# A causal attention stage whose longest row tile is turned by DMA instead of by TensorE

## The chip, the cores and the metric

The kernel runs on one core of a Trainium2 chip. The metric is the device time of one execution in microseconds (us), lower is better. The core has five engines that work through their own instruction lists in order and wait for each other only through semaphores: TensorE (PE: matmuls, and PEld: its weight loads), VectorE (DVE), ScalarE (ACT), GpSimd (POOL) and SyncE (SP), whose queue issues nearly all DMAs here.

## The reference

Two layers over 1024 tokens of width 1024, batch 1. Layer 0 mixes a pooling branch and a short convolution. Layer 1 is attention with 16 heads, and it is the part that matters here:

```python
def causal_attention(q, k, v):          # q, k: 16 heads of 96; v: 16 heads of 64
    def block(i):                       # 8 blocks of 128 query rows
        s = jnp.einsum('bqhd,bkhd->bhqk', qb, k) * scale
        s = jnp.where(k_idx[None, :] <= q_idx[:, None], s, -jnp.inf)
        p = jax.nn.softmax(s, axis=-1)
        return jnp.einsum('bhqk,bkhd->bqhd', p, v)
...
    o = causal_attention(q, k, v)
    return x + (o * jax.nn.silu(z)) @ w_out
```

Values are float32. The kernel reaches that precision with pairs of 16-bit numbers: a value is split into a high half (the value rounded to float16) and a low half (what the rounding lost), and a product takes two or three passes.

## The kernel before, in words

The program has a front part (layer 0 and the input projections), then the projections of queries, keys and values, then attention, then the output projection. Attention works on 16 heads one after the other; a head has 8 query tiles of 128 rows. By the causal mask tile i needs only the first i+1 blocks of 128 keys, so tile 7 is 1024 columns wide and tile 0 is 128. Within a head the tiles come in the order `ORDER = (7, 3, 6, 2, 5, 1, 4, 0)`; n counts tiles over all heads (n = 8h is tile 7 of head h), so big tiles (i of 4 and more, `heads_probs_big`) and small ones (`heads_probs_small`) alternate. A big tile's row is cut into two pieces of up to 512 columns, a small tile has one.

One tile passes through these stages, each written on its engine's list:

- PE, `score_tile(n)` (L111 to L113): scores into PSUM, three passes.
- DVE, `maxima(n)` (L2487): scales, adds the mask, writes the row to SBUF (`heads_probs_big` or `_small`) and takes the row's maximum.
- ACT, `exponentials(n)` (L2357): the exponential in place, with the row's sum.
- PE, `transposes(n, k)` (L2729): piece k in blocks of 128x128 float32, against the identity, into one of three PSUM banks.
- ACT, `high(n, k)` (L2366): the piece from PSUM to `heads_pt_hi`, float16.
- DVE, `low(n, k)` (L2495): PSUM minus that, to `heads_pt_lo`, float16.
- PE, `product(n, k)` (L2747, L2748): both halves against V, two matmuls for each block of 128.

The order is written out by hand, and no scheduler changes it. In step n PE does the scores of tile n+2, the transposes of tile n and the product of tile n-2, ACT does `high` of tile n and then `exponentials` of tile n+2, and DVE does `maxima` of tile n+2 and then `low` of tile n:

```python
for n in range(N + BEHIND):                     # ACT
    for k in range(len(pieces(tile_of(n)[1]))):
        high(n, k)
    exponentials(n + AHEAD)                     # AHEAD = 2
...
for n in range(N + BEHIND + TURN_LAG + 1):      # DVE
    maxima(n + AHEAD)
    for k in range(len(pieces(tile_of(n)[1]))):
        low(n, k)
```

After each two heads PE also turns their outputs (`turn`, L2756, eight transposes of `heads_o_pair`) and DVE multiplies them into the gate (L2508). ACT copies each group of four tiles' outputs out of PSUM (`copy_out`, L2373), and POOL sums and scales them (L2642, L2647), splits V (L2633, L2635) and, from the middle of attention on, prepares operands of the output projection. SP issues for head h, once the scores of head h-2 are done, two DMA transposes that bring the keys and the queries of the head from DRAM (`load_k`, L2275, `load_q`, L2278), then weights, V and stores.

## Time and profile before

| | |
|---|---|
| median of 3 runs | 964.08 us (963.87 to 965.23) |
| the profiled execution | 965.27 us, its span 963.4 us |
| granted TensorE clock over the span | 0.998 |
| attention, about 656 to 881 us of the span | 226 us |
| PE, DVE, ACT busy over the whole span | 98%, 84%, 60% |
| DMA | 103.67 MB |

The span runs from the first to the last instruction; 1.9 us of the profiled execution's time lie around it. Busy time is the time in which at least one instruction of an engine is under way. Durations of matmuls overlap their neighbours (their ends are modelled), and the last 0.1 us of a DVE or ACT instruction overlaps the next one; what an instruction costs its queue is therefore read from the start of one instruction to the start of the next, called its slot below. In a row of the timeline "x2" merges two neighbours.

### The profile page before, as it was taken

The page shows a single profiled execution, that of the slowest core. Times are in us where ns is not written, and L with a number is a line of the kernel's source. Part 1 is how long each engine was busy: PE and PEld are TensorE (multiplying, and loading weights), DVE is VectorE, ACT ScalarE, POOL GpSimd, SP SyncE. Part 2 cuts the span into 40 slices and gives each one's busy share as a digit, 9 for nine tenths or more (in the row PEclk, how much of TensorE's full clock was granted, in tenths as well). Part 3 has the DMA queues.
Part 4 walks back from the last instruction along what each step waited for, and adds up shares of the span by engine and source line. Part 5 has one row for each costly group of instructions (what it writes and reads, how often), then busy time and mean ns, then how long its engine had stood idle before and what let it go on. Part 6 is the DMA issues. An engine that isn't in the chain of part 4 may idle for free.

```text
span 963.4 us, 16135 instructions
## 1 busy us (share of the span) xinstructions
PE 947.1 (98%) x5830; PEld 668.9 (69%) x5830; DVE 813.5 (84%) x1410; ACT 579.5 (60%) x1076; POOL 376.3 (39%) x425
## 2 busy tenths in 40 slices
PE   9999999999999999999998999999999999999998
PEld 7788544444688888544456999997778888887443
DVE  5798899899865579989786799998999999998763
ACT  7434544434444354555646788866999999998230
POOL 0002243222000002235402567867673589897220
PEclk9999999999999999999999999999999999999999
DMA  9320431111055422423024164557665766460231
GB/s 305 46 58 23 110 86 46 44 45 45 1 183 163 134 66 66 132 88 79 9 72 132 44 208 146 203 176 203 116 161 146 172 153 111 92 175 2 88 110 66
DMA packets 165343, 103.67 MB, mean 108 GB/s; under 512 B 75272, under 2 KB 149520, under 8 KB 165008
## 3 DMA queue, kind: packets, MB, share of 16 engines
q1 hardware_dynamic: 159216, 102.25, 37.8%
q10 hardware_dynamic: 6048, 0.39, 0.5%
q8 instruction: 47, 0.77, 0.3%
q14 instruction: 32, 0.26, 0.1%
HBM read 56.48 MB, written 29.36 MB: 89 GB/s over the span
## 4 chain that ended last, share of the span: by engine, by line
PE 64%; DVE 24%; POOL 5%; issue 4%; ACT 3%; DVEq 0%; POOLq 0%; ACTq 0%
PE banks L111 18%; PE banks L113 18%; PE banks L112 17%; PE banks L2729 5%; PE banks L2747 2%; DVE heads_y L2478 2%; PE banks L2748 1%; DVE heads_x L2473 1%; DVE heads_x L2474 1%; DVE heads_ss L2520 1%; DVE front_lt L1231 1%; ACT front_set_b L722 1%; DVE heads_probs_big L2487 1%; DVE front_l L1231 1%; DVE heads_last_y L2478 1%
## 5 line engine op out<-in xcount | busy, mean ns | idle before, releaser
L2495 DVE TENSOR_TENSOR heads_pt_lo<-banks,heads_pt_hi 128x512 f16<-128x512 f32 (+2 forms) x192 | 102.1, 554 | 11.3 <-ACT heads_pt_hi L2366 7.0
L2366 ACT ACTIVATE heads_pt_hi<-banks 128x512 f16<-128x512 f32 (+2 forms) x192 | 88.3, 484 | 4.9 <-PE banks L2729 4.6
L2747 PE MATMUL banks<-heads_v,heads_pt_hi 128*128 128x128 f16 x576 | 74.5, 220 | 0.0
L2729 PE MATMUL banks<-ident,heads_probs_big 128*128 128x128 f32 x416 | 69.1, 279 | 1.4 <-ACT heads_probs_big L2357 1.3
L2748 PE MATMUL banks<-heads_v,heads_pt_lo 128*128 128x64 f16 x576 | 69.5, 193 | 0.0
L2487 DVE CUSTOM_DVE_ANT_0 heads_probs_big<-banks,heads_mask,score_scale 128x1024 f32<-128x1024 f32 (+1 forms) x64 | 68.5, 1071 | 0.9
L2357 ACT ACTIVATE heads_probs_big<-heads_probs_big,heads_neg_max 128x1024 f32<-128x1024 f32 (+1 forms) x64 | 63.4, 991 | 5.5 <-DVE heads_neg_max L2487 3.6
L111 PE MATMUL banks<-front_act_hi,front_w_hi 128*128 128x512 f32 x160 | 63.9, 399 | 0.3 <-DVE front_w_lo L951 0.3
L111 PE MATMUL banks<-heads_k_t,heads_q_t 96*128 96x512 f16 (+2 forms) x192 | 62.9, 327 | 0.9 <-DVE heads_neg_max L2487 0.9
L113 PE MATMUL banks<-front_act_hi,front_w_lo 128*128 128x512 f32 x160 | 62.4, 390 | 0.0
L112 PE MATMUL banks<-front_act_lo,front_w_hi 128*128 128x512 f32 x160 | 62.3, 389 | 0.0
L112 PE MATMUL banks<-heads_k_t,heads_q_t 96*128 96x512 f16 (+2 forms) x192 | 62.3, 324 | 0.0
L113 PE MATMUL banks<-heads_k_t,heads_q_t 96*128 96x512 f16 (+2 forms) x192 | 61.5, 325 | 0.0
L626 POOL TENSOR_TENSOR front_left_first<-front_raw_first 128x512 f32<-128x512 f32 x1 | 1.3, 1297 | 147.8 <-DVE front_lt L1231 147.8
L2747 PEld LDWEIGHTS banks<-heads_v,heads_pt_hi 128*128 128x128 f16 x576 | 54.2, 99 | 0.7
L2748 PEld LDWEIGHTS banks<-heads_v,heads_pt_lo 128*128 128x128 f16 x576 | 51.3, 98 | 2.3
L2729 PEld LDWEIGHTS banks<-ident,heads_probs_big 128*128 128x128 f32 x416 | 46.7, 141 | 7.7 <-DVE heads_pt_lo L2495 3.3
L111 PE MATMUL banks<-front_y_hi,front_w_hi 128*128 128x512 f32 x128 | 50.0, 391 | 0.0
L113 PE MATMUL banks<-front_y_hi,front_w_lo 128*128 128x512 f32 x128 | 49.8, 389 | 0.0
L112 PE MATMUL banks<-front_y_lo,front_w_hi 128*128 128x512 f32 x128 | 49.8, 389 | 0.0
L626 POOL TENSOR_TENSOR front_x<-front_raw 128x512 f32<-128x512 f32 x7 | 9.7, 1380 | 85.6 <-DVE front_set_b L1090 36.5
L2357 ACT ACTIVATE heads_probs_small<-heads_probs_small,heads_neg_max 128x512 f32<-128x512 f32 (+1 forms) x64 | 35.9, 561 | 7.4 <-DVE heads_neg_max L2487 6.6
(488 smaller groups left out, 3099.7 us busy)
## 6 DMA issues: line engine op xcount, KB each, us to landing
qk_scratch<-heads_y SPq DMA_DIRECT2D x22, 512.0 KB, 3.6
front_x<-in_x_t SPq DMA_DIRECT2D x16, 512.0 KB, 5.2
front_raw<-in_w_in_ab SPq DMA_DIRECT2D x14, 512.0 KB, 5.1
qk_scratch<-heads_last_y SPq DMA_DIRECT2D x10, 512.0 KB, 3.6
front_w<-in_w_out_ab SPq DMA_DIRECT2D x8, 512.0 KB, 3.7
x_scratch<-front_x SPq DMA_DIRECT2D x8, 512.0 KB, 4.0
v_scratch<-heads_v SPq DMA_DIRECT2D x32, 128.0 KB, 3.0
heads_v_st<-v_scratch SPq DMA_DIRECT2D x8, 512.0 KB, 5.2
```

The lines of the kernel that those rows point to most:

```text
L111: nc.tensor.matmul(out, w_hi, a_hi, start=first, stop=False, skip_group_check=resumed)
L112: nc.tensor.matmul(out, w_hi, a_lo, start=False, stop=False, skip_group_check=resumed)
L113: return nc.tensor.matmul(out, w_lo, a_hi, start=False, stop=last, skip_group_check=resumed)
L1231: nc.vector.scalar_tensor_tensor(right_split(c, part, 1), right_source(c, part), later_scale[:, 0:1], right_split(c, part, 0), ALU.mult, A ...
L2357: nc.scalar.activation(row, row, ACT.Exp, bias=neg_max[:, h % 2, i:i + 1], scale=-1.0, accum_out=total[:, h % 2, i:i + 1]).then_inc(exp_do ...
L2366: nc.scalar.activation(pt_hi[:, q % PIECES, :width], t_ps[:, banks[("piece", n, k)] % 3, :width], ACT.Copy).then_inc(pt_high, 1)
L2478: nc.vector.tensor_tensor(y_slot(w)[:, :, :, P:P + QKH], x_slot(w), y_slot(w)[:, :, :, :QKH], ALU.subtract).then_inc(y_low, 1)
L2487: nc.vector.tensor_tensor_reduce(probs(n, 0, width), scores(i, 0, width), mask[:, S - width:], score_scale[:], 3e38, ALU.add, ALU.min, neg ...
L2495: nc.vector.tensor_tensor(pt_lo[:, q % PIECES, :width], t_ps[:, banks[("piece", n, k)] % 3, :width], pt_hi[:, q % PIECES, :width], ALU.sub ...
L2729: last = nc.tensor.transpose(t_ps[:, b, r * P:(r + 1) * P], probs(n, j * P, (j + 1) * P), ident[:])
L2747: nc.tensor.matmul(out, pt_hi[:, q % PIECES, blk], v2[e][:, j, :], start=(j == 0), stop=False)
L2748: last = nc.tensor.matmul(out[:, :VH], pt_lo[:, q % PIECES, blk], v2[e][:, j, :VH], start=False, stop=(j == i))
```

## The change

For tile 7 of each head but the first (n = 8, 16, ..., 120, fifteen tiles) the four stages after the exponential are replaced. ACT casts the whole row, 1024 columns, from SBUF to SBUF (`big_high`, to `out.big[0]`), right after the row's exponential. DVE subtracts it from the row, SBUF to SBUF (`big_low`, to `out.big[1]`), one step later. SP issues a DMA transpose for each half (`turn_big`), from SBUF to SBUF, behind the loads of the keys and queries of the next head. PE multiplies the result with V in one go (`big_product`) five steps after the tile's own step, where it was two and in two pieces. The ring of transposed pieces has 5 places where it had 6, the buffers of the output projection are placed elsewhere, the four residual rows load only after the last scores, and POOL's waits within its own operations use one shared semaphore.

```diff
+        def turn_big(h):
+            for part, made in enumerate((out.big_high, out.big_low)):
+                sp.wait_ge(made, h)
+                if h > 1:
+                    sp.wait_ge(out.big_done, h - 1)
+                sp.dma_start_transpose(out.big_t[part][:], out.big[part][:].rearrange("p b k -> p (b k)")
+                                       ).then_inc(out.big_in, 16)
...
             sp.wait_ge(s_ready, NT * (h - 1))
             load_k(h)
             load_q(h)
+            turn_big(h - 1)
...
+        turn_big(HEADS - 1)
+        sp.wait_ge(s_ready, N)
         for m in range(out.PLACES_OF_ROWS):
             out.load_residual(sp, m)
...
+        def big_high(n):
+            h = n // NT
...
+            act.wait_ge(exp_done, n + 1)
+            act.wait_ge(out.big_in, 32 * (h - 1))
+            nc.scalar.activation(out.big[0][:].rearrange("p b k -> p (b k)"), probs(n, 0, S), ACT.Copy).then_inc(out.big_high, 1)
...
             if n + AHEAD < N:
                 exponentials(n + AHEAD)
+                if by_queue(n + AHEAD):
+                    big_high(n + AHEAD)
...
-            if n >= 4:
-                dve.wait_ge(pt_ready, piece_no(n - 4, len(pieces(tile_of(n - 4)[1])) - 1) + 1)
+            if n >= 4 and by_queue(n - 4):
+                dve.wait_ge(out.big_low, (n - 4) // NT)
+            elif n >= 4:
+                dve.wait_ge(pt_ready, piece_base[n - 3])
...
+        def big_low(n):
+            h = n // NT
+            dve.wait_ge(out.big_high, h)
+            dve.wait_ge(out.big_in, 32 * (h - 1))
+            nc.vector.tensor_tensor(out.big[1][:].rearrange("p b k -> p (b k)"), probs(n, 0, S),
+                                    out.big[0][:].rearrange("p b k -> p (b k)"), ALU.subtract).then_inc(out.big_low, 1)
...
             if n < N:
-                for k in range(len(pieces(tile_of(n)[1]))):
+                for k in range(len(parts(n))):
                     low(n, k)
+                if by_queue(n + 1) and n + 1 < N:
+                    big_low(n + 1)
                 if n % 4 == 3:
                     inverse(n // 4)
...
+        def big_product(n):
+            h = n // NT
+            e, o_part = h % 2, o_ps[:, n // 4 % 2, o_slot(NT - 1), :]
+            pe.wait_ge(out.big_in, 32 * h)
+            for j in range(NT):
+                nc.tensor.matmul(o_part, out.big_t[0][:, j], v2[e][:, j, :], start=(j == 0), stop=False)
+                last = nc.tensor.matmul(o_part[:, :VH], out.big_t[1][:, j], v2[e][:, j, :VH], start=False, stop=(j == NT - 1))
+            last.then_inc(out.big_done, 1)
...
+                if k == 0 and by_queue(big) and big < N:
+                    big_product(big)
```

`by_queue(n)` is true for n = 8, 16, ..., 120, and `parts(n)` is then empty. Two places of the lists show what moves.

DVE, at the border of two heads, the change (`heads_probs_big` of 128x1024 is tile 7, of 128x896 tile 6, `heads_probs_small` of 128x512 tile 3, of 128x384 tile 2; the rows called ISA are `maxima` and the reading of its maximum). The list starts after `maxima` of tile 7, with `low` of tile 4 of the head before:

```order
L2528 TENSOR_TENSOR heads_pt_lo<-banks,heads_pt_hi 128x512
L2528 TENSOR_TENSOR heads_pt_lo<-banks,heads_pt_hi 128x128
L2520 ISA heads_probs_small,heads_neg_max<-banks,heads_mask,score_scale 128x512
L2520 ISA heads_neg_max 128x1
L2528 TENSOR_TENSOR heads_pt_lo<-banks,heads_pt_hi 128x128
L2535 TENSOR_TENSOR out_big_lo<-heads_probs_big_260,out_big 128x1024
L2543 RECIPROCAL heads_inv<-heads_total 128x2x2
L2520 ISA heads_probs_big_270,heads_neg_max<-banks,heads_mask,score_scale 128x896
L2520 ISA heads_neg_max 128x1
L2520 ISA heads_probs_small,heads_neg_max<-banks,heads_mask,score_scale 128x384
L2520 ISA heads_neg_max 128x1
L2528 TENSOR_TENSOR heads_pt_lo<-banks,heads_pt_hi 128x512
```

The same place before:

```order
L2495 TENSOR_TENSOR heads_pt_lo<-banks,heads_pt_hi 128x512
L2495 TENSOR_TENSOR heads_pt_lo<-banks,heads_pt_hi 128x128
L2487 ISA heads_probs_small,heads_neg_max<-banks,heads_mask,score_scale 128x512
L2487 ISA heads_neg_max 128x1
L2495 TENSOR_TENSOR heads_pt_lo<-banks,heads_pt_hi 128x128
L2503 RECIPROCAL heads_inv<-heads_total 128x2x2
L2487 ISA heads_probs_big_267,heads_neg_max<-banks,heads_mask,score_scale 128x896
L2487 ISA heads_neg_max 128x1
L2495 TENSOR_TENSOR heads_pt_lo<-banks,heads_pt_hi 128x512 x2
L2487 ISA heads_probs_small,heads_neg_max<-banks,heads_mask,score_scale 128x384
L2487 ISA heads_neg_max 128x1
L2495 TENSOR_TENSOR heads_pt_lo<-banks,heads_pt_hi 128x512
```

The two `low` of tile 7 are gone from between the maxima of tiles 6 and 2, and the new subtraction stands ahead of the maxima of tile 6.

ACT, the same border, the change: exponential of tile 7, the cast, `high` of tile 0 of the head before, the exponentials of tiles 3 and 6, `high` of tile 3, the exponential of tile 2:

```order
L2375 ACTIVATE heads_probs_big_260,heads_total<-heads_probs_big_260,heads_neg_max 128x1024
L2394 ACTIVATE out_big<-heads_probs_big_260 128x1024
L2384 ACTIVATE heads_pt_hi<-banks 128x128
L2375 ACTIVATE heads_probs_small,heads_total<-heads_probs_small,heads_neg_max 128x512
L2375 ACTIVATE heads_probs_big_270,heads_total<-heads_probs_big_270,heads_neg_max 128x896
L2384 ACTIVATE heads_pt_hi<-banks 128x512
L2375 ACTIVATE heads_probs_small,heads_total<-heads_probs_small,heads_neg_max 128x384
```

The same place before:

```order
L2357 ACTIVATE heads_probs_big_257,heads_total<-heads_probs_big_257,heads_neg_max 128x1024
L2366 ACTIVATE heads_pt_hi<-banks 128x128
L2357 ACTIVATE heads_probs_small,heads_total<-heads_probs_small,heads_neg_max 128x512
L2366 ACTIVATE heads_pt_hi<-banks 128x512 x2
L2357 ACTIVATE heads_probs_big_267,heads_total<-heads_probs_big_267,heads_neg_max 128x896
L2366 ACTIVATE heads_pt_hi<-banks 128x512
L2357 ACTIVATE heads_probs_small,heads_total<-heads_probs_small,heads_neg_max 128x384
```

The cast has come in front of `high` of tile 0, and the two casts of tile 7's pieces have gone.

## Rows read from the trace of the kernel before

**Rows 1.** The page: the span, and busy time of PE and DVE.

```profile
span 963.4 us, 16135 instructions
PE 947.1 (98%) x5830; PEld 668.9 (69%) x5830; DVE 813.5 (84%) x1410; ACT 579.5 (60%) x1076; POOL 376.3 (39%) x425
```

**Rows 2.** Windows: attention, then two neighbouring heads of it.

```profile
655.90:881.50 225.60, 221.62 (x2360) 176.22 (x2359) 211.78 (x515) 207.04 (x493) 172.62 (x199) 1.00 0.59 137
773.40:786.50 13.10, 13.10 (x147) 10.52 (x145) 12.35 (x30) 12.60 (x32) 12.63 (x12) 1.00 0.56 122
786.50:800.40 13.90, 13.90 (x153) 11.23 (x152) 13.32 (x32) 12.48 (x31) 10.94 (x11) 1.00 0.64 150
```

**Rows 3.** Timeline of DVE: start us, us, instruction [idle before <-releaser].

```profile
773.44 1.28 DVE L2487 CUSTOM_DVE_ANT_0 heads_probs_big<-banks,heads_mask,score_scale 128x1024 f32<-128x1024 f32 x1
...
774.65 0.88 DVE L2495 TENSOR_TENSOR heads_pt_lo<-banks,heads_pt_hi 128x512 f16<-128x512 f32 x2
...
775.45 0.74 DVE L2487 CUSTOM_DVE_ANT_0 heads_probs_small<-banks,heads_mask,score_scale 128x512 f32<-128x512 f32 x1
...
776.21 0.29 DVE L2495 TENSOR_TENSOR heads_pt_lo<-banks,heads_pt_hi 128x128 f16<-128x128 f32 x1
...
776.60 1.15 DVE L2487 CUSTOM_DVE_ANT_0 heads_probs_big<-banks,heads_mask,score_scale 128x896 f32<-128x896 f32 x1
...
777.68 1.49 DVE L2495 TENSOR_TENSOR heads_pt_lo<-banks,heads_pt_hi 128x512 f16<-128x512 f32 x2
...
779.09 0.61 DVE L2487 CUSTOM_DVE_ANT_0 heads_probs_small<-banks,heads_mask,score_scale 128x384 f32<-128x384 f32 x1
...
779.99 0.69 DVE L2495 TENSOR_TENSOR heads_pt_lo<-banks,heads_pt_hi 128x512 f16<-128x512 f32 x1 [0.28 <-ACT heads_pt_hi L2366]
...
786.51 1.28 DVE L2487 CUSTOM_DVE_ANT_0 heads_probs_big<-banks,heads_mask,score_scale 128x1024 f32<-128x1024 f32 x1
...
789.78 0.29 DVE L2495 TENSOR_TENSOR heads_pt_lo<-banks,heads_pt_hi 128x128 f16<-128x128 f32 x1
```

**Rows 4.** Timeline of ACT, the same columns and heads.

```profile
774.77 1.15 ACT L2357 ACTIVATE heads_probs_big<-heads_probs_big,heads_neg_max 128x1024 f32<-128x1024 f32 x1
...
775.92 0.25 ACT L2366 ACTIVATE heads_pt_hi<-banks 128x128 f16<-128x128 f32 x1
...
778.34 1.03 ACT L2357 ACTIVATE heads_probs_big<-heads_probs_big,heads_neg_max 128x896 f32<-128x896 f32 x1
...
779.37 0.58 ACT L2366 ACTIVATE heads_pt_hi<-banks 128x512 f16<-128x512 f32 x1
...
787.84 1.15 ACT L2357 ACTIVATE heads_probs_big<-heads_probs_big,heads_neg_max 128x1024 f32<-128x1024 f32 x1
```

**Rows 5.** Timeline of PE, the same columns, an earlier and the same head.

```profile
764.11 0.63 PE L2729 MATMUL banks<-ident,heads_probs_big 128*128 128x128 f32 x4
...
764.58 0.22 PE L2747 MATMUL banks<-heads_v,heads_pt_hi 128*128 128x128 f16 x1
...
771.47 0.39 PE L2729 MATMUL banks<-ident,heads_probs_small 128*128 128x128 f32 x2
...
771.94 0.38 PE L111 MATMUL banks<-heads_k_t,heads_q_t 96*128 96x512 f16 x1
```

**Rows 6.** Sources and tiles: durations ns min/median/max of SBUF operations on DVE and ACT.

```profile
L960 DVE TENSOR_TENSOR front_w_lo<-front_w,front_w_hi x15: 1211/1218/1471, 58.0 to 372.2; 128x1024 fp32r<-128x1024 f32 x15
L1816 ACT ACTIVATE heads_dump<-gate x8: 1055/1056/1122, 526.6 to 594.4; 128x1024 bf16<-128x1024 f32 x8
```

**Rows 7.** Groups by form, 520 to 680 us, POOL busy too: busy us, mean ns.

```profile
L2478 DVE TENSOR_TENSOR heads_y<-heads_x,heads_y 128x768 f16<-128x768 f32 x16 | 19.2, 1203 | 2.1 <-ACT heads_y L2351 2.1
```

**Rows 8.** Timeline of SP's queue in the next head, and landing times of the keys.

```profile
784.72 1.91 SPq L2275 DMA_TRANSPOSE heads_k_t<-qk_scratch  x1
786.68 2.20 SPq L2278 DMA_TRANSPOSE heads_q_t<-qk_scratch  x1
DMA to landing us min/median/max: 4.3/5.1/6.4
```

More of the change, by code:

```diff
@@ L1716, in __init__ @@
         self.w_row, self.w_size, self.w_scale, self.unscale = [field(self.OUT_PAIRS) for _ in range(4)]
-        sum_places = (joint.rstd_at, ring_at + tile, ring_at + 4 * tile)
-        self.sums = [[at(f"sums{q}_{n}", block, F32, place + (n if q or n < 3 else 2) * half)[:]
-                      for n in range(4) if q or n != 2]
+        sum_places = (spare + 6 * 1024, joint.rstd_at, ring_at + 4 * tile)
+        self.sums = [[at(f"sums{q}_{n}", block, F32, place + (n if q == 2 or n < 3 else 2) * half)[:]
+                      for n in range(4) if q == 2 or n != 2]
                      for q, place in enumerate(sum_places)]
-        self.sums[0].insert(2, self.quarter_of(0, 1, 0))
+        for q in range(2):
+            self.sums[q].insert(2, self.quarter_of(q, 1, 0))
         self.left = [at(f"left{q}", [P, FORMS, 2] + block[1:], F16, w_place + q * FORMS * half) for q in range(self.OUT_PAIRS)]
@@ L1877, in pool_t @@
         one, other = self.t_terms(c, f, raw, raw)
-        self.nc.gpsimd.tensor_tensor(raw, one, other, ALU.subtract).then_inc(self.t_staged, 1)
-        pool.wait_ge(self.t_staged, done + 1)
-        self.nc.gpsimd.tensor_copy(hi, raw).then_inc(self.t_cast, 1)
-        pool.wait_ge(self.t_cast, done + 1)
+        link(self.nc.gpsimd.tensor_tensor(raw, one, other, ALU.subtract))
+        link(self.nc.gpsimd.tensor_copy(hi, raw))
         self.nc.gpsimd.tensor_tensor(lo, raw, hi, ALU.subtract).then_inc(self.t_split, 1)
@@ L2188, in pieces, with by_queue, parts @@
         return [range(b, min(b + 4, i + 1)) for b in range(0, i + 1, 4)]
-    PER_HEAD = sum(len(pieces(i)) for i in range(NT))
+    def by_queue(n):
+        return n > 0 and n % NT == 0
+    def parts(n):
+        return [] if by_queue(n) else pieces(tile_of(n)[1])
+    piece_base = [0]
+    for n in range(N):
+        piece_base.append(piece_base[-1] + len(parts(n)))
     def piece_no(n, k):
-        h, p = divmod(n, NT)
-        return PER_HEAD * h + sum(len(pieces(ORDER[x])) for x in range(p)) + k
+        return piece_base[n] + k
     def turn_step(pair, c):
@@ L2367, in high @@
                                  ACT.Copy).then_inc(pt_high, 1)
+        def big_high(n):
+            h = n // NT
+            if h == 1:
+                for e in range(VSLOTS):
+                    act.wait_ge(v_stored[e], 16 * len(range(e, UNITS, VSLOTS)))
+            act.wait_ge(exp_done, n + 1)
+            act.wait_ge(out.big_in, 32 * (h - 1))
+            nc.scalar.activation(out.big[0][:].rearrange("p b k -> p (b k)"), probs(n, 0, S), ACT.Copy).then_inc(out.big_high, 1)
         def copy_out(g):
+            if g % 2 == 0 and g:
+                act.wait_ge(out.big_done, g // 2)
             act.wait_ge(pv_done, piece_no(4 * g + 3, len(pieces(ORDER[(4 * g + 3) % NT])) - 1) + 1)
@@ L2412, in scalar @@
             if n < N:
-                for k in range(len(pieces(tile_of(n)[1]))):
+                for k in range(len(parts(n))):
                     high(n, k)
@@ L2541, in vector @@
             if n < N:
-                for k in range(len(pieces(tile_of(n)[1]))):
+                for k in range(len(parts(n))):
                     low(n, k)
+                if by_queue(n + 1) and n + 1 < N:
+                    big_low(n + 1)
                 if n % 4 == 3:
@@ L2691, in gpsimd @@
                 for n in range(2):
-                    out.pool_t(pool, c, 2 * late + n)
+                    out.pool_t(pool, link, c, 2 * late + n)
                 if not late:
-                    out.pool_gate(pool, c + 2)
+                    out.pool_gate(pool, link, c + 2)
             if h == 11:
@@ L2735, in product @@
             q = piece_no(n, k)
-            if n % NT == 0 and k == 0:
+            first = 1 if by_queue(n - 1) else 0
+            if n % NT == first and k == 0:
                 pe.wait_ge(v_low, h + 1)
-            if n % 4 == 0 and k == 0:
+            if n % 4 == (first if n % NT < 2 else 0) and k == 0:
                 if g >= 2:
@@ L2801, in tensor @@
             old = n - BEHIND
-            new_pieces = len(pieces(tile_of(n)[1])) if n < N else 0
-            old_pieces = len(pieces(tile_of(old)[1])) if 0 <= old < N else 0
+            new_pieces = len(parts(n)) if n < N else 0
+            old_pieces = len(parts(old)) if 0 <= old < N else 0
+            big = n - BIG_BEHIND
             if n == N:
```

54 lines of the change are left out of this document (27 added, 27 removed).

## The prediction

> **What bounds the kernel now.** I read the page first: the span is 963.4 us and PE is busy in 98% of it [rows 1]. Then the windows of attention, because the change touches nothing else: 225.6 us, of which PE is busy 221.6, DVE 211.8 and ACT 207.0 [rows 2]. The two windows of one head each are what to look at. A head in which no outputs are turned lasts 13.1 us, one in which they are 13.9, and in both PE is busy all of it. But DVE is busy 12.35 and 13.32 of them, and ACT 12.60 and 12.48 [rows 2]. So PE sets the pace, with DVE only 0.6 to 0.75 us of a head behind it. A change that takes time from PE can give at most those 0.6 to 0.75 us a head before DVE is the bound, and it gives less if it makes DVE wait.
>
> So the third view is the timeline of DVE through one head border [rows 3]. The reader is to see how dense it is: maxima of tile 7 at 773.44, `low` of tile 4 at 774.65, maxima of tile 3 at 775.45, `low` of tile 0 at 776.21, maxima of tile 6 at 776.60, the two `low` of tile 7 at 777.68, maxima of tile 2 at 779.09, and only then a wait of 0.28, for ACT. Each `low` needs a cast of ACT, and that cast stands behind an exponential that needs a maximum of DVE. The two engines hand work to and fro, and it goes without waits only because each has other work while the other has the tile. For tile 7 that other work is what the change removes or lengthens.
>
> **PE.** Removed: eight transposes in each of 15 tiles. Four take a slot of 0.47 us (764.11 to 764.58) [rows 5], so 0.94 a head and 14.1 in all. The products are the same sixteen matmuls, moved: nothing. This is a gain only where PE is the bound.
>
> **ACT.** Removed: two casts of 512 columns out of PSUM, with slots of 0.48 (779.37 to the next instruction) to 0.62 [rows 3, 4]. Added: one cast of 1024 columns in SBUF. The nearest row is a one-input operation over the same shape, 1.056 us [rows 6], and with 0.1 of overlap a slot of 0.96. Its sum stays; its place doesn't: it now stands between the exponential of tile 7 and `high` of tile 0.
>
> **DVE.** Removed: the two `low` of tile 7, a slot of 1.41 (777.68 to 779.09), and the wait of 0.28 behind them [rows 3]. Added: a subtraction of 1024 columns in SBUF. The nearest row is 1.218 us for 1024 columns of float32 and a rounded copy [rows 6], a slot of 1.14. Upper bound: while POOL works, 768 columns took 1.203 on average [rows 7] where that rate gives 0.91, a factor of 1.32, so up to 0.38 more. I take 1.14, since the maker of that row is the same operation.
>
> **Wait X, in front of `low` of tile 0.** Before, ACT begins the exponential of tile 7 at 774.77 and `high` of tile 0 at 775.92 [rows 4], and DVE finds it done at 776.21 [rows 3]. With the cast between, ACT is done at 774.77 + 1.15 + 0.96 + 0.25 and some 0.05 for the semaphore, 777.18. DVE waits 0.97 us. In a head with turned outputs DVE has a gate product more and comes to that `low` at 789.78 [rows 3], while ACT began at 787.84 [rows 4] and is done at 790.25: 0.47. Queued behind it are the new subtraction and the maxima of tile 6.
>
> **Wait Y, in front of `low` of tile 3.** Before, between the maxima of tile 6 and of tile 2 DVE had the 1.41 us of tile 7's pieces, and ACT had time for the exponential of tile 6 (1.03, 778.34 to 779.37) and `high` of tile 3 (0.62 until DVE takes it at 779.99) [rows 3, 4]. Now DVE goes from the maxima of tile 6 straight to those of tile 2 (0.62) and then needs `high` of tile 3, which is behind that exponential. From the end of the maxima: 0.12 until ACT starts (774.65 to 774.77 for tile 7) + 1.03 + 0.62 = 1.77, less 0.62, is 1.15 us of waiting.
>
> **Wait Z, in front of the next tile 7.** PE's product of tile 7 (eight blocks; three take 0.25 of the 0.47 us between 771.47 and 771.94, so 0.66) now stands right before the 1024 columns of scores, in step n+5 [rows 5]. DVE wants these scores. Between 0, if PE is ahead, and 0.66; I take 0.3, since PE has to catch up after each wait of DVE.
>
> **The sum.** No outputs turned: -1.41 - 0.28 + 1.14 + 0.97 + 1.15 + 0.3 = +1.87 a head. Outputs turned: the same with 0.47 for X, +1.37. The turned outputs of a pair fall into heads 3, 5, ..., 15, seven of the fifteen: 8 x 1.87 + 7 x 1.37 = 24.6 us. Made against the profiled execution (965.27, its span 963.4) that is 989.9, and against the median of 964.08, which lies 1.2 below it, 988.7. I predict 989.
>
> **The transposes in the DMA queue.** The sum needs them in time. Counted from the start of the maxima of tile 7: the cast ends at 3.4 (774.77 + 1.15 + 0.96 - 773.44) and the subtraction at 5.1 (777.18 + 0.20 + 1.14 - 773.44). SP is free by then: the two loads of the next head are issued from 784.72 to 788.88 [rows 8], 2.4 after maxima that start at 786.51 [rows 3], one period of 13.07 on. A load of 1024x256 takes 4.3 to 6.4 us from issue to landing, 5.1 in the middle [rows 8], and each new transfer has half its bytes: the low half has landed 10.2 to 11.5 after the maxima. PE wants it where it ends the transposes of tile 1, 1.75 us before the next such maxima (771.69 against 773.44) [rows 3, 5]: with the stretched period at 13.07 + 1.57 - 1.75 = 12.9. Hidden, by 1.4 to 2.7 us; in a head with turned outputs the product comes 0.4 later still. No row shows a transpose whose source is SBUF, so how long it takes is the open point, and its bounds are in the rivals.
>
> The Trainium skill speaks against the change here: "VectorE: DVE Perf Modes", section "The three transpose paths", gives a block of 128x128 1309 ns by the DMA crossbar and 390 ns on TensorE. By it the sixteen blocks of a tile would take 20.9 us one after the other, land 11.4 us late in each head, and make about 1160 us, an estimate from that page. The trace doesn't agree for the same instruction from DRAM: a load holds sixteen such blocks and has landed after 5.1 us [rows 8]. No row shows an SBUF source. I give it 1 in 100.
>
> **What costs nothing.** The loads of weights and V now stand behind both transposes in SP's queue, some 3 us later than their 788.88; V is for a head that starts one period later, and without that cover each us late would be a us of PE. The ring of 5 pieces holds the four of two tiles and one more. POOL's semaphores change their names, not their number of waits. The residual rows are wanted only by the additions after attention, under the first output products.
>
> **Rivals.**
> - *PE stays the bound* (faster, 950): the waits X and Y are filled. It decides at X + Y + Z = 0.55 a head (1.41 + 0.28 - 1.14); below that DVE gains. For it: PE's 100% [rows 2]. Against it: DVE's list is in order, and X alone is 0.97. 964 - 14.1 = 950. 7 in 100.
> - *Nothing is left of it* (962 to 966): X and Y are half as long, because ACT gets ahead in the rest of the head. Against it: both start at a maximum of DVE, so ACT can't be ahead. 5 in 100.
> - *The transposes come late as well* (997 to 1040): if the two don't overlap, the low half lands at 3.4 + 2 x 5.1 = 13.6, which is 0.7 late in a head without turned outputs and 0.3 in the other, about 8 us in all, 997; with 6.4 each, 3.2 late and 48 more, 1037. The skill's figure would be beyond. 10 in 100, with 1010 in the middle.
> - *The forecast*: 78 in 100. Its own range: X and Y each 0.2 shorter and Z 0 takes 10.5 off, 978; Z 0.66 and POOL's 0.38 add 11.1, 1000.
>
> **Range and chances.** 975 to 1008 holds the forecast's range with a little on both sides and the nearer half of the late transposes; left out are the faster and the equal case and the later half, with some of the forecast's tails. About 2 us (0.2%) is what a measurement of this kernel can tell from no change. Faster 0.07, same 0.05, slower 0.88.
>
> **What the profile after would show.** PE no longer busy all of a head window, a head of about 14.9 us without and 15.3 with turned outputs; on DVE a wait of about 1 us for ACT before `low` of tile 0 and another before `low` of tile 3; the new subtraction near 1.2 us; PE waiting for DVE's maxima and ACT's exponentials, not for the transfers. I am wrong if DVE's waits for ACT stay as short as now and heads fall under 13.1 us, or if PE sits in front of the product of tile 7.

## The result, and the profile after

The changed kernel takes 1003.04 us (median of 4, 1001.92 to 1003.54), the kernel before beside it on the same chip 964.62 (963.87 to 965.23): a ratio of 1.0396, 95% interval 1.0384 to 1.0408. It is 38.4 us slower. Forecast were 24.6 us more, 989, and a range of 975 to 1008, which holds it. The profiled execution has a span of 1000.1 us, against 963.4 [rows 1]: 36.7 more. It is less than 38.4 because the profiled execution of the changed kernel was its fastest, 1001.92, and that of the kernel before was slower than its median, 965.27.

The page of the changed kernel, the span, the busy time, and four of the five groups of PE, DVE and ACT in attention in front of which most idle time stands (last two numbers: idle us before the group, and the releaser of most of it; the fifth is ACT's `high`, 11.4 us, nearly all for PE's transposes):

```profile
span 1000.1 us, 15913 instructions
PE 952.4 (95%) x5710; PEld 663.4 (66%) x5710; DVE 815.0 (81%) x1395; ACT 579.9 (58%) x1061; POOL 386.3 (39%) x425
...
L2528 DVE TENSOR_TENSOR heads_pt_lo<-banks,heads_pt_hi 128x512 f16<-128x512 f32 (+3 forms) x162 | 81.6, 529 | 36.2 <-ACT heads_pt_hi L2384 33.2
L111 PE MATMUL banks<-heads_k_t,heads_q_t 96*128 96x512 f16 (+2 forms) x192 | 64.8, 338 | 24.1 <-DVE heads_neg_max L2520 23.7
L2375 ACT ACTIVATE heads_probs_big<-heads_probs_big,heads_neg_max 128x1024 f32<-128x1024 f32 (+1 forms) x64 | 63.4, 990 | 41.4 <-DVE heads_neg_max L2520 39.2
L2520 DVE CUSTOM_DVE_ANT_0 heads_probs_big<-banks,heads_mask,score_scale 128x1024 f32<-128x1024 f32 (+1 forms) x64 | 68.6, 1072 | 11.1 <-PE banks L113 10.7
```

PE is no longer busy all the time, and the three engines wait for one another: DVE's `low` for ACT, ACT and PE for DVE's `maxima`, and the `maxima` for PE's scores. Nobody in this list waits for a transfer.

The windows of one head each, from one start of the maxima of tile 7 to the next (they answer to [rows 2]):

```profile
758.32:773.62 15.30, 13.03 (x138) 9.42 (x137) 12.08 (x29) 12.83 (x30) 8.70 (x9) 1.00 0.84 170
773.62:789.52 15.90, 13.79 (x146) 10.37 (x145) 13.28 (x32) 12.55 (x29) 5.94 (x8) 1.00 0.76 167
789.52:806.18 16.66, 14.10 (x138) 10.72 (x137) 13.01 (x30) 12.45 (x29) 16.15 (x12) 0.90 0.69 126
806.18:822.86 16.68, 15.01 (x146) 11.76 (x145) 13.48 (x32) 12.46 (x29) 10.71 (x11) 0.90 0.74 162
```

The first number behind the window is its length, the next four busy times are those of PE, weight loads, DVE and ACT, the fifth is POOL's, and then stands the granted clock. A head takes 15.30 us without and 15.90 with turned outputs, where it took 13.07 and 14.00. But half of the heads are longer still, 16.2 to 16.8, and in them TensorE was granted only 0.89 to 0.90 of its clock.

The timeline of DVE in the second of these heads, with turned outputs (it answers to [rows 3]):

```profile
773.62 1.28 DVE L2520 CUSTOM_DVE_ANT_0 heads_probs_big<-banks,heads_mask,score_scale 128x1024 f32<-128x1024 f32 x1 [0.76 <-PE banks L113]
...
777.48 0.29 DVE L2528 TENSOR_TENSOR heads_pt_lo<-banks,heads_pt_hi 128x128 f16<-128x128 f32 x1 [0.50 <-ACT heads_pt_hi L2384]
777.68 1.22 DVE L2535 TENSOR_TENSOR out_big_lo<-heads_probs_big,out_big 128x1024 f16<-128x1024 f32 x1
...
780.55 0.61 DVE L2520 CUSTOM_DVE_ANT_0 heads_probs_small<-banks,heads_mask,score_scale 128x384 f32<-128x384 f32 x1
781.09 0.08 DVE L2520 DVE_READ_ACCUMULATOR2_ANT heads_neg_max<- 128x1 f32 x1
782.31 0.69 DVE L2528 TENSOR_TENSOR heads_pt_lo<-banks,heads_pt_hi 128x512 f16<-128x512 f32 x1 [1.15 <-ACT heads_pt_hi L2384]
```

All three waits of the forecast are there: Z in front of the maxima of tile 7 (0.76), X in front of `low` of tile 0 (0.50; 1.10 in the head before it, without turned outputs), and Y in front of `low` of tile 3 (1.15). X in the head before it:

```profile
762.18 0.29 DVE L2528 TENSOR_TENSOR heads_pt_lo<-banks,heads_pt_hi 128x128 f16<-128x128 f32 x1 [1.10 <-ACT heads_pt_hi L2384]
```

ACT shows why, in the head of the timeline above:

```profile
774.95 1.15 ACT L2375 ACTIVATE heads_probs_big<-heads_probs_big,heads_neg_max 128x1024 f32<-128x1024 f32 x1
776.00 0.19 ACT L2375 ACTIVATION_READ_ACCUMULATOR heads_probs_big<-heads_probs_big,heads_neg_max 128x1 f32 x1
776.22 1.06 ACT L2394 ACTIVATE out_big<-heads_probs_big 128x1024 f16<-128x1024 f32 x1
777.19 0.26 ACT L2384 ACTIVATE heads_pt_hi<-banks 128x128 f16<-128x128 f32 x1
...
780.66 1.04 ACT L2375 ACTIVATE heads_probs_big<-heads_probs_big,heads_neg_max 128x896 f32<-128x896 f32 x1 [2.52 <-DVE heads_neg_max L2520]
```

The new cast (L2394) stands between the exponential of tile 7 and `high` of tile 0, for which DVE waits. Then, behind the exponential of tile 3, ACT itself sits idle for 2.52 us until the maxima of tile 6.

### The profile page after: what moved, and what is told of

Read it like the earlier page. It is cut to its first block, busy times and chain, and to the rows that moved or that the text cites. A ratio compares the mean times of both kernels' runs of the same rounds, so it can differ in the third digit from the quotient of the medians.

```text
span 1000.1 us, 15913 instructions
## 1 busy us (share of the span) xinstructions
PE 952.4 (95%) x5710; PEld 663.4 (66%) x5710; DVE 815.0 (81%) x1395; ACT 579.9 (58%) x1061; POOL 386.3 (39%) x425
## 4 chain that ended last, share of the span: by engine, by line
PE 53%; DVE 25%; POOL 9%; issue 8%; ACT 4%; DVEq 0%; POOLq 0%; ACTq 0%
PE banks L111 16%; PE banks L113 16%; PE banks L112 16%; PE banks L2772 3%; DVE heads_probs_big L2520 2%; DVE heads_y L2509 2%; DVE heads_x L2504 1%; DVE heads_x L2505 1%; PE banks L2791 1%; POOL out_t_hl L1880 1%; POOL out_pool_stage L1878 1%; DVE heads_ss L2560 1%; DVE front_lt L1231 1%; POOL heads_o_sum L2684 1%; POOL out_gate_hl L1862 1%
## 5 line engine op out<-in xcount | busy, mean ns | idle before, releaser
L2528 DVE TENSOR_TENSOR heads_pt_lo<-banks,heads_pt_hi 128x512 f16<-128x512 f32 (+3 forms) x162 | 81.6, 529 | 36.2 <-ACT heads_pt_hi L2384 33.2
L2384 ACT ACTIVATE heads_pt_hi<-banks 128x512 f16<-128x512 f32 (+3 forms) x162 | 71.0, 463 | 11.4 <-PE banks L2772 11.0
L2791 PE MATMUL banks<-heads_v,heads_pt_hi 128*128 128x128 f16 x456 | 59.7, 223 | 0.0
L2772 PE MATMUL banks<-ident,heads_probs_big 128*128 128x128 f32 x296 | 52.6, 302 | 4.9 <-ACT heads_probs_big L2375 3.5
L2792 PE MATMUL banks<-heads_v,heads_pt_lo 128*128 128x64 f16 x456 | 55.6, 195 | 0.0
L2684 POOL TENSOR_TENSOR heads_o_sum<-heads_o_raw 128x256 f32<-128x256 f32 x32 | 24.3, 759 | 59.7 <-ACT heads_o_raw L2402 58.9
L2772 PEld LDWEIGHTS banks<-ident,heads_probs_big 128*128 128x128 f32 x296 | 37.2, 153 | 12.9 <-DVE heads_pt_lo L2528 4.9
L2791 PEld LDWEIGHTS banks<-heads_v,heads_pt_hi 128*128 128x128 f16 x456 | 43.9, 101 | 1.7
L2792 PEld LDWEIGHTS banks<-heads_v,heads_pt_lo 128*128 128x128 f16 x456 | 41.5, 99 | 2.7
L111 PEld LDWEIGHTS banks<-heads_k_t,heads_q_t 96*128 96x128 f16 x192 | 19.2, 100 | 36.2 <-DVE heads_neg_max L2520 27.7
```

The costliest lines, as they stand in the source:

```text
L111: nc.tensor.matmul(out, w_hi, a_hi, start=first, stop=False, skip_group_check=resumed)
L2384: nc.scalar.activation(pt_hi[:, q % PIECES, :width], t_ps[:, banks[("piece", n, k)] % 3, :width], ACT.Copy).then_inc(pt_high, 1)
L2528: nc.vector.tensor_tensor(pt_lo[:, q % PIECES, :width], t_ps[:, banks[("piece", n, k)] % 3, :width], pt_hi[:, q % PIECES, :width], ALU.sub ...
L2684: nc.gpsimd.tensor_tensor(o_sum[:, g % 2], raw[:, :, :VH], raw[:, :, VH:], ALU.add).then_inc(o_summed, 1)
L2772: last = nc.tensor.transpose(t_ps[:, b, r * P:(r + 1) * P], probs(n, j * P, (j + 1) * P), ident[:])
L2791: nc.tensor.matmul(out, pt_hi[:, q % PIECES, blk], v2[e][:, j, :], start=(j == 0), stop=False)
```

## Experiments

All kernels were timed beside the kernel before, whose medians were 964.2 to 965.2 us there. "Heads" are the distances between the maxima of tile 7, first without and then with turned outputs. Of each kernel the shortest that recur are given, at a granted clock of 1.00; other heads of the same kernel are longer, and where that matters it is said.

### Both new instructions at the old places

```
 scalar:  for k in range(len(parts(n))): high(n, k)
+         if by_queue(n): big_high(n)
          exponentials(n + AHEAD)
-         if by_queue(n + AHEAD): big_high(n + AHEAD)
 vector:  for k in range(len(parts(n))): low(n, k)
-         if by_queue(n + 1) and n + 1 < N: big_low(n + 1)
+         if by_queue(n): big_low(n)
```

> The cast of the whole row goes to the place in ACT's list where the two casts of tile 7's pieces stood (before the exponential of tile 6), the subtraction to the place in DVE's list where the two low stood (after the maxima of tile 6). Transposes by the queue, their bytes and PE's savings stay. Theory A (DVE and ACT wait for each other because the cover is gone: X in front of low of tile 0, Y in front of low of tile 3): both waits fall under 0.4 us, a head comes down from 15.3/15.9 to 13.0 to 13.6 / 13.9 to 14.2, PE stays busy enough to keep its clock at 1.00, and the time is 960 to 974. Theory B (transposes from SBUF cost the time, by late landing or by loading the DMA engines): the halves are made 1.5 to 2 us later than in the changed kernel, so it gets no better, 1000 or more, and PE waits in front of the product of tile 7.

979.54 us (978.12 to 981.08), ratio 1.0151 (1.013 to 1.0172). Heads of 13.73 and 14.34, X and Y are gone, the clock is 1.00 in each head:

```profile
719.75:733.48 13.73, 12.66 (x138) 9.47 (x137) 12.29 (x30) 13.07 (x31) 5.99 (x7) 1.00 0.69 151
733.48:747.82 14.34, 13.67 (x146) 10.33 (x145) 13.28 (x31) 13.18 (x31) 4.29 (x5) 1.00 0.88 205
```

Most of the loss, 23.5 of 38.4 us, was in where the two instructions stand. But the expectation was too low by 6 at its upper end: without X and Y a head still isn't shorter than before. Nine of 14 heads are longer than these two, up to 15.11 us. Part of that is the subtraction: it takes 1.22 us in the undisturbed heads and up to 2.13 in others, 3.9 us more in all fifteen together than at 1.22.

### Only the subtraction at its old place

The second half of the diff above, alone.

> Only the subtraction goes back to its old place on DVE; the cast stays right behind the exponential. Theory A: Y (1.15 a head) is filled by the subtraction, X (0.5 to 1.0 a head) stays. 15 heads x 1.15 less, some 17 us, and more where PE's clock no longer falls: 975 to 988. Theory B: the low half is made 2 us later, nothing gained or slower: 1003 or more.

983.08 us (981.27 to 984.5), ratio 1.0184 (1.0165 to 1.0202), inside the 975 to 988 expected. Y is down to 0.20, X is still 1.10 and 0.50; heads of 14.33 and 14.93:

```profile
721.57:735.90 14.33, 13.03 (x138) 9.43 (x137) 12.17 (x29) 13.17 (x31) 6.39 (x8) 1.00 0.66 148
```

Y was worth 0.97 a head, 14.5 in all, where 1.15 was expected, and with it the drops of the clock went.

### Only the cast one step later

```
 scalar:  for k in range(len(parts(n))): high(n, k)
+         if by_queue(n + 1) and n + 1 < N: big_high(n + 1)
          exponentials(n + AHEAD)
-         if by_queue(n + AHEAD): big_high(n + AHEAD)
```

> Only the cast moves, by one place: behind high of tile 0 in ACT's list. The subtraction stays in front of the maxima of tile 6. Theory A: X moves from low of tile 0 to the subtraction and is 0.2 shorter at most, Y stays at 1.15: 998 to 1003, nearly no change. A rival within A, that X comes from the place of the cast alone: 15 x 0.5 to 1.0 less, 988 to 995.

998.71 us (995.85 to 1000.01), ratio 1.0343 (1.032 to 1.0365). X is gone, but without turned outputs DVE now waits 0.65 for the cast itself, in front of the subtraction. Heads of 14.95 and 15.55, 0.35 less. So this move alone gives a third of the 0.97 that X was put at, since the wait partly moves to the next hand-over, as theory A had it. With the subtraction out of the way the same move of the cast gives more, as the fifth experiment shows.

### PE filled where it was idle

```
 score_tile:
-    for kc in range(i // 4 + 1):
+    for kc in [0] * (3 if by_queue(n - 3) else 0) + list(range(i // 4 + 1)):
```

> The changed kernel with three more rounds of the scores of tile 2 (three passes of 384 columns each, 1.47 us in all, the same values written again) where PE sat idle for 1.57 us before the scores of tile 5. It is more work for PE. Theory C (the 12 us beyond the forecast are half the granted clock, which fell to 0.50 for some 3.5 us in seven heads, after PE had been idle in them): the clock stays at 1.00, the heads of 16.1 to 16.8 us come down to 15.3 and 15.9, and the time is 994 to 999, faster with more work. If the clock is only a symptom: 1003 or slower, by up to 0.2 us a head.

999.38 us (998.37 to 1000.5), ratio 1.0354 (1.0337 to 1.0371): 3.7 us less than the changed kernel, with more work on PE, and just above the 994 to 999 expected. No head has a lower clock any more. The head with the largest gain and the two that went the other way:

```profile
694.83:710.13 15.30, 14.30 (x147) 10.39 (x146) 12.17 (x29) 13.07 (x31) 14.33 (x20) 1.00 0.80 189
710.13:727.52 17.39, 15.25 (x155) 11.23 (x154) 14.86 (x31) 13.07 (x31) 8.39 (x12) 1.00 0.67 151
...
821.95:838.23 16.28, 14.30 (x147) 10.39 (x146) 13.06 (x30) 12.55 (x29) 15.44 (x16) 1.00 0.76 129
```

The first was 16.24 and is 15.30, the clean value. The other two were 16.82 and 15.40: in them DVE is busy 14.86 and 13.06, and the subtraction takes 2.71 and 2.19 us, where it takes 1.22 at 777.68 in the changed kernel, with POOL idle. In the head of 17.39 an operation of POOL on 768 columns begins at 714.18:

```profile
714.20 2.71 DVE L2535 TENSOR_TENSOR out_big_lo<-heads_probs_big,out_big 128x1024 f16<-128x1024 f32 x1
```

So two things, seen apart here, make a head longer than 15.30 or 15.90: a lower clock behind PE's idle time, and a subtraction that runs beside POOL.

### The cast ahead of the exponential, the subtraction at its old place

The cast as in the third experiment and the subtraction as in the second.

> The changed kernel with both new instructions at other places: the cast stands right behind `high` of the tile before (tile 0), ahead of the exponential of tile 3 and not behind that of tile 7's neighbour, and the subtraction stands where the two `low` of tile 7 stood. Theory A (the places of the two make the waits X and Y; the sum of ACT's and DVE's work alone does not): X and Y stay away as in the run with the old places (979.5), and `low` of tile 0 no longer waits at all while the exponentials behind it start 0.96 us later; the hand-over after tile 7 is the best of the three, so 974 to 980. Rival (the busy time of ACT, 13.04 of 13.70 us in a head of that run, is now what bounds): the order inside ACT changes nothing, 979 to 982.

980.73 us (977.96 to 981.92), ratio 1.0161 (1.0143 to 1.0179). Heads of 13.38 and 14.34:

```profile
722.68:736.06 13.38, 12.45 (x138) 9.47 (x137) 12.29 (x30) 13.05 (x31) 6.36 (x8) 1.00 0.70 163
```

Beside the second experiment only the cast has moved, and X is gone with no wait for the cast in its place: 0.95 a head without turned outputs (14.33 to 13.38) and 0.59 with them (14.93 to 14.34). That is the whole of X, 0.97 and 0.47 in the forecast. Beside the old places (the first experiment) the head without turned outputs gains 0.35, and others lose it again (one has 16.34), so theory A isn't borne out in the time: the medians, 980.7 and 979.5, don't differ clear of their spread.

### The high half turned twice

```
 turn_big:
+    for again in range(2 - part):
+        if again: sp.wait_ge(out.big_in, 48 * h - 32)
         sp.dma_start_transpose(...)
```

> The changed kernel, but the high half of each tile 7 is transposed twice by the queue, the second time when the first has landed; the low half goes behind both. Theory A (the transposes are hidden: the low half lands about 5 us before PE's product of it): both halves land some 3 us later, still about 2 us early, so no change, 1001 to 1005. Rival (part of the missing 13 us is the queue: PE or the later loads wait for it in heads that the chain of waits does not show): each head later by up to 3 us, 1008 to 1045.

1001.59 us (1000.3 to 1004.5), ratio 1.0385 (1.0365 to 1.0406), as the changed kernel. In the changed kernel the product starts 7.1 to 9.0 us after the low half is issued. Here it starts 3.2 to 7.0 us after it, on average 3 us less, and it waited for it 0.3 us in two heads together. So the transfers are hidden in the changed kernel: landing takes 3.0 to 3.4 of its 7.1 us or more.

### PE's product one step earlier

```
-    AHEAD, BEHIND, TURN_LAG, PIECES, BIG_BEHIND = 2, 2, 5, 5, 5
+    AHEAD, BEHIND, TURN_LAG, PIECES, BIG_BEHIND = 2, 2, 5, 5, 4
```

> The changed kernel with PE's product of tile 7 one step earlier, at n+4 and not n+5, so that it no longer stands right before the 1024 columns of scores of the next tile 7. Theory A (wait Z is the product, 0.33 to 0.96 us a head): DVE finds those scores ready and the product runs in PE's idle time, 15 heads x 0.35 to 0.7 = 5 to 10 us less, 992 to 998. Rival (PE comes to those scores late because it has caught up after DVE's waits, and everything in front of them counts, wherever the product stands): no change, 1001 to 1005.

1005.64 us (1004.1 to 1007.31), ratio 1.0424 (1.0408 to 1.0439). Theory A falls: heads of 15.31 and 15.90, nothing gained, and nine heads with a lower clock where seven had one. PE waits 0.40 for the exponential of tile 5 at the start of step n+4 and from there works without a gap to the scores of the next tile 7; the product counts at either place.

### The product in front of that wait

`BIG_BEHIND` is 3, and the waits for V and for the copied outputs stand in front of the product of tile 7.

> The changed kernel with PE's product of tile 7 in step n+3 and not n+5 (the waits for V and for the copied outputs move with it). With the product at n+4 nothing was gained, because PE works without a gap from its wait for the exponential of tile 5 (the transposes at 769.48, in front of the old place and the new) to the scores of the next tile 7, so that 0.66 us counts in either. Step n+3 lies in front of that wait. Theory A (Z is the product inside that stretch): the waits in front of the maxima of tile 7 fall by 0.3 to 0.6 and the heads by 0.3 to 0.5, 996 to 1000, if the low half, which lands 8.4 us after the maxima, is in time. Rival (what PE gains there it loses in front of the scores of tile 1, or at the transfer): 1001 to 1008.

1002.39 us (1001.06 to 1006.14), ratio 1.039 (1.0368 to 1.0412). Where the clock is 1.00 the heads are 0.68 shorter, as much as the product takes; the whole isn't:

```profile
742.00:758.68 16.68, 15.00 (x146) 11.75 (x145) 13.48 (x31) 13.17 (x31) 6.06 (x7) 0.90 0.97 189
758.68:773.30 14.62, 12.79 (x138) 9.41 (x137) 12.08 (x29) 12.23 (x30) 8.01 (x9) 1.00 0.82 180
773.30:788.51 15.21, 13.54 (x146) 10.32 (x145) 13.27 (x31) 12.44 (x30) 5.60 (x8) 1.00 0.81 175
```

Nine of 14 heads now have a clock of 0.80 to 0.90, where seven had. So Z is the product, and its price 0.68 rather than 0.3. What it gives back is lost in the nine heads; the longest of them, 18.48 us, also has a subtraction of 3.06 us beside POOL.

### POOL makes both, in six heads

`by_queue` holds only in heads 4, 5 and 12 to 15. There POOL makes cast and subtraction, between the two scalings of the outputs of the head before.

> The queue turns tile 7 only in six heads (4, 5 and 12 to 15), those in which POOL has idle time, and in them POOL makes both the cast (1.04 us for 1024 columns in the trace of before) and the subtraction (2.14 us): ACT and DVE only lose work there. All other heads are as before, but with the ring of five pieces. Theory A (a head is bound by the hand-over between maxima, exponentials, transposes, `high` and `low` as much as by the busiest engine, so work taken away turns into waits, Y above all): the six heads last 12.8 to 13.9 as before, 961 to 966. Rival (the busiest engine bounds: PE loses 0.94 of 13.1, DVE 1.41 of 12.35, ACT 1.1 of 12.6): a head of 12.2 to 13.1, six times 0.9 less, 957 to 960.

989.11 us (987.62 to 989.75), ratio 1.0254 (1.0237 to 1.0271). Heads 12 to 14 lasted 19.9 to 21.4 us: POOL came to them late (the maxima waited 19.6 us for its subtraction in all), so that was a wrong choice of heads, and the total speaks for neither theory. All heads that don't use the queue last what they did, 13.07 and 14.01, so the ring of five pieces costs nothing. Heads 4 and 5 are the test. They last 13.52 and 14.18, 13.11 and 14.28 before, although ACT and DVE got nothing new. (Head 4 also has a wait of 0.59 for POOL's subtraction; head 5 has none.) The wait Y stands there in full:

```profile
737.37 0.09 DVE L2525 DVE_READ_ACCUMULATOR2_ANT heads_neg_max<- 128x1 f32 x1
738.60 0.69 DVE L2533 TENSOR_TENSOR heads_pt_lo<-banks,heads_pt_hi 128x512 f16<-128x512 f32 x1 [1.15 <-ACT heads_pt_hi L2390]
```

### POOL makes the cast alone

Heads 1 to 5; the subtraction on DVE at its old place.

> The queue turns tile 7 only in heads 1 to 5; in them POOL makes the cast (1.04 us) and DVE the subtraction, at the place of the two removed `low`, so that Y is filled and ACT has two casts less and none more. The other heads are as before. Theory A (with the old places it is ACT, 13.04 of 13.70 us, that makes the heads longer than before): heads 4 and 5, where POOL is free, last 12.6 to 13.0 and 13.6 to 14.1 where before they last 13.11 and 14.28, the whole 962 to 966. Rival (the hand-over decides, not ACT's work, and POOL's cast is late): 13.4 and 14.4 or more, 966 to 972.

982.4 us (979.2 to 983.18), ratio 1.0171 (1.0152 to 1.0189). In heads 1 and 2 (24.7 and 19.1 us) POOL was late, which puts the total above both expectations. In heads 4 and 5 DVE had no wait for POOL's cast. They last 13.55 and 14.33, and 13.38 and 14.34 with the cast on ACT (the fifth experiment). Theory A falls: ACT's load is not what makes the head.

### Nothing added

```
 big_high (and big_low alike):
+    if h == 1: nc.scalar.activation(out.big[0] ...).then_inc(out.big_high, 1)
+    else: act.sem_inc(out.big_high, 1)
```

> The changed kernel without what it adds on ACT and DVE: the cast and the subtraction are made in head 1 alone, and in the heads behind it the queue turns what stands there, so the outputs of the later heads leave out their own tile 7. All that is removed stays removed, all semaphores and transfers stay. Theory A (wait Y comes from the removal alone: DVE has nothing between the maxima of tile 6 and tile 2): heads of 13.3 to 13.7 without turned outputs and 14.0 to 14.4 with, as in the two heads that POOL served; 965 to 972, so no gain even if both new instructions cost nothing. Rival (sums of the engines: PE is the bound again, 0.94 a head less): 950 to 954.

971.08 us (970.32 to 971.84), ratio 1.0062 (1.0045 to 1.0079). Behind head 1 each head has eight transposes, two casts and two subtractions less and no new work on PE, ACT, DVE or POOL (the queue's transposes stay), and the kernel is still 6 us slower than before. 2.35 of these are head 1, in which both new instructions are still made; the next thirteen are 3.5 us slower together, on average 0.4 each without and 0.1 with turned outputs. Two of them:

```profile
776.96:790.44 13.48, 12.88 (x138) 9.43 (x137) 11.05 (x29) 11.60 (x28) 13.01 (x12) 1.00 0.87 155
790.44:804.61 14.17, 13.62 (x146) 10.34 (x145) 12.05 (x30) 11.72 (x28) 11.12 (x11) 1.00 0.87 190
```

```profile
776.96 1.28 DVE L2523 CUSTOM_DVE_ANT_0 heads_probs_big<-banks,heads_mask,score_scale 128x1024 f32<-128x1024 f32 x1 [0.77 <-PE banks L113]
...
780.03 0.29 DVE L2531 TENSOR_TENSOR heads_pt_lo<-banks,heads_pt_hi 128x128 f16<-128x128 f32 x1 [0.31 <-ACT heads_pt_hi L2384]
...
783.24 0.69 DVE L2531 TENSOR_TENSOR heads_pt_lo<-banks,heads_pt_hi 128x512 f16<-128x512 f32 x1 [1.15 <-ACT heads_pt_hi L2384]
```

DVE is busy 11.05 of 13.48 us. It lost 1.41 of work and a wait of 0.28, and it waits 0.77 + 0.31 + 1.15 instead. These waits have different sources. Y, 1.15, is what the removal uncovers. The 0.77 is Z: PE's product still stands in step n+5, where it was worth 0.68 a head. No run leaves out both the new work and that move, so whether the removal by itself gains something isn't shown.

### Old places, and the product inside PE's wait

The first experiment, with `BIG_BEHIND` 4 and `big_product` ahead of `transposes` in its step.

> The version with both new instructions at the old places (979.5), and PE's product of tile 7 in step n+4 in front of the transposes of that step, that is inside PE's wait of 0.66 us for the exponential of tile 5 (in that version the low half has landed at 757.5, the wait is from 757.4 to 758.0). Theory A (the product costs only where PE has no wait in front of it): 0.35 to 0.6 less in each of 15 heads, heads of 13.2 and 13.9, 971 to 975. Rival (the transfer is now just late, so PE waits for it and the head gains nothing, or the wait in front of the maxima was the turned outputs and not the product): 977 to 983. Neither reaches the 965 of the kernel before.

984.23 us (982.28 to 985.89), ratio 1.0204 (1.0185 to 1.0223). The shortest heads fell to 13.44 and 13.88, 0.29 and 0.46 less, near the 0.35 to 0.6 of theory A. But the total is above both expectations, since the product has come too close to the transfer:

```profile
PE banks L2801 <- DMA out_big_t_lo<-out_big_lo: 5.3, 5, 3.1
```

In the head that starts at 692.96 PE waited 3.1 us for the low half: SP issued it only at 701.43, behind the two loads of the next head (694.32 to 699.98). That head lasts 17.89 us. Another, with a wait of 2.01 for a `low` before outputs are turned, lasts 18.49. Both are at a clock of 0.90 to 0.91, and the whole is worse than with the product a step later. In the head of 13.44 PE waited 0.35 for the low half too.

## Why the prediction was right, and where its sizes were off

*What bounds the kernel, and the sign.* Right. PE's 14.1 us are worth nothing, and the three waits stand where the forecast put them. That the range holds the time is luck in part. By its own terms the forecast reached 978 to 1000, and 1003 lies above that; the range went on to 1008 for late transposes, and none was late. Heads of 14.9 and 15.3 us were forecast, and the undisturbed ones last 15.3 and 15.9.

*Wait X.* Right in its place and size: 1.10 and 0.50 measured, 0.97 and 0.47 forecast. As a term of the sum it was right too: with the subtraction at its old place, moving the cast out of its way gives 0.95 and 0.59 a head (the second experiment beside the fifth). The sum only doesn't say what one gets by taking X away while the subtraction still stands behind the cast: 0.35, in the third experiment.

*Wait Y.* 1.15 forecast, 1.15 measured, to the digit. It comes from the removal, not from what is added: it is there in full when POOL does the new work and when nobody does. Filling it again gives 0.97 a head, with a rest of 0.20 left.

*Wait Z.* Right in its place, mis-sized: "I take 0.3". The trace has 0.33 and 0.76, and removing it gives 0.68, the whole product. The upper bound of the prediction, 0.66, was the value. PE can't catch up after DVE's waits, as the prediction assumed it half could: it works without a gap from its last wait on. With 0.68 for Z the forecast's sum is 2.25 and 1.75 a head, and 2.33 and 1.75 were measured in undisturbed heads: Z is the one term of the sum that was clearly mis-sized.

*The subtraction.* 1.215 to 2.055 us with a median of 1.314 (by DVE's own row in this trace), against 1.218; POOL's share came out in some heads and is more than the 0.38 that was the bound there:

```profile
L2535 DVE TENSOR_TENSOR out_big_lo<-heads_probs_big,out_big x15: 1215/1314/2055, 682.1 to 906.9; 128x1024 f16<-128x1024 f32 x15
```

*The transposes in the queue.* Hidden, as forecast, and by more. In this trace they land 3.0 to 3.4 us after issue (one high half 4.4), not 5.1, so the low half of the head above, issued at 778.98, is there at about 782.1, 8.5 after the maxima, where 10.2 to 11.5 was forecast. The Trainium skill, "VectorE: DVE Perf Modes", section "The three transpose paths", has 1309 ns for a block of 128x128 on the crossbar path; for the eight blocks of one half one after the other that is 10.5 us, an estimate from that page. The trace doesn't agree:

```profile
L2295 SPq DMA_TRANSPOSE out_big_t_lo<-out_big_lo x15: 1231/1232/1262, 683.5 to 908.6; - x15
...
DMA to landing us min/median/max: 3.0/3.1/3.4
```

*The rivals.* PE as the bound: excluded, even with nothing added (971 and not 950). Nothing left of it: no. Late transposes: not here; they show once the product is moved up to them.

*The missing 12 us* of the span (36.7 measured, 24.6 forecast) are in two parts of about the same size. First, the four heads without turned outputs at full clock are 2.33 longer than theirs before on average (15.30, 15.30, 15.40, 15.40 against 13.11, 12.84, 13.06, 13.06), forecast 1.87; the three with them and the last head 1.75, forecast 1.37: 8 x 0.46 + 7 x 0.38 = 6.3. That is Z above all. Second, the other seven heads are 20.4 us longer than before, where 4 x 2.33 + 3 x 1.75 = 14.6 is the measure of the undisturbed ones: 5.9 more. Some 2.5 of these are longer work of DVE, 1.7 of it the subtraction beside POOL, an estimate from the windows: DVE is busy 0.2 to 0.9 us longer in six of the seven than in the undisturbed ones (13.01 against 12.08, 13.48 against 13.28). The rest, some 3.4, is the clock; filling PE gave 3.7. The prediction had no term for the clock, and only a bound of its range had one for POOL.

How it falls is to be seen in windows of 1 us of the head from 789.52 (the second number is PE's busy time, the one behind POOL's is the granted clock):

```profile
793.52:794.52 1.00, 0.37 (x4) 0.36 (x4) 1.00 (x2) 0.53 (x2) 1.00 (x2) 1.00 0.73 163
794.52:795.52 1.00, 0.38 (x5) 0.22 (x3) 1.00 (x1) 0.00 (x0) 1.00 (x2) 1.00 1.12 211
795.52:796.52 1.00, 0.00 (x0) 0.00 (x0) 1.00 (x3) 0.00 (x0) 1.00 (x1) 1.00 0.18 40
796.52:797.52 1.00, 0.69 (x3) 0.31 (x4) 0.79 (x4) 0.71 (x1) 0.92 (x2) 0.94 0.70 137
797.52:798.52 1.00, 1.00 (x6) 0.77 (x5) 0.06 (x1) 1.00 (x4) 1.00 (x1) 0.50 0.81 147
798.52:799.52 1.00, 1.00 (x7) 1.00 (x6) 1.00 (x2) 1.00 (x4) 0.92 (x2) 0.50 0.79 200
799.52:800.52 1.00, 1.00 (x6) 0.81 (x5) 0.97 (x3) 1.00 (x4) 1.00 (x2) 0.50 0.94 280
```

PE waits for DVE, whose subtraction takes 2.06 us in this head; PE is busy 0.75 of 3 us; and when it has work again its clock is 0.50, 1.2 GHz and not 2.4, for the next 3 us and more.

## What stays open

Why one or two heads of 15 grow by 2 us and more with the new instructions at or near their old places isn't settled: in them PE waits 1.5 to 2.8 us for a `low` before it turns outputs, in one head of the first experiment (its last) and in two each of the fifth and the last. How the 5.9 us split into clock and DVE is an estimate. No arrangement that was run beats the kernel before; the best that keeps the result has 979.5. Not run is the product in step n+3 together with both new instructions at the old places.

## What to carry to other kernels

Where engines hand a tile on in small steps, the work of one on the other tiles is what covers the latency of the next hand-over. Work removed there can turn into a wait of almost its own size: DVE's 1.41 us a head became a wait of 1.15. So before moving work off an engine, look which wait it covers, and test it by leaving the work out altogether, as in the run with nothing added: with the rest of the change in its place, that run is the most that a cheaper replacement can give. Here it took away 0.94 us of PE, 1.1 of ACT and 1.41 of DVE a head, and a head was 0.1 to 0.4 us longer on average. That includes what PE's product costs at its new place, 0.68 a head where it was measured. And if something has to be added, put it where the removed work stood.

## What was not expected of the hardware

- A transpose of 1024 columns of 16 bits by the queue from SBUF to SBUF takes 1.23 us to issue and lands 3.0 to 3.4 us after issue (one of 30 after 4.4), mostly less than the 4.3 to 6.4 us of the loads from DRAM [rows 8] with twice the bytes.
- The granted clock falls to 0.50 inside a head in which PE is busy for 82% to 90% of the time, as in the windows above: PE was busy 0.75 of the 3 us before, and the half clock came when it had work again.
- A subtraction of DVE with both operands in SBUF goes from 1.22 to 2.06 and 2.71 us beside POOL's work, and POOL's cast beside it from 1.04 to 2.03 us. The rows look as if the two took turns rather than shared:

```profile
792.43 2.13 POOL L1856 TENSOR_TENSOR out_plain_hl<-out_plain,out_plain_hl 128x1024 f16<-128x1024 f32 x1
793.59 2.06 DVE L2535 TENSOR_TENSOR out_big_lo<-heads_probs_big,out_big 128x1024 f16<-128x1024 f32 x1
794.51 2.03 POOL L1861 CAST out_gate_hl<-gate 128x1024 f16<-128x1024 f32 x1
```

The subtraction ends 1.09 us after the POOL operation in front of it (795.65 against 794.56), and so does the one of 2.71 us in the fourth experiment (716.91 against 715.82); the cast ends 0.89 us after the subtraction.
